# Moving a modulation product beside the first two down projections, and placing TensorE's operands at multiples of 2,048 bytes

## What is computed

```
h  = x + short_conv_mixer(rms_norm(x))          # in: 1024 -> 3*1024, width-3 convolution, out: 1024 -> 1024
h  = h + conv_ffn(rms_norm(h))                  # up 1024 -> 2*2816, convolution, silu(g)*u, down 2816 -> 1024
h  = h + mla_attention(rms_norm(h), shared_latent_kv(...), cos, sin)   # 8 heads
h  = h + conv_ffn(rms_norm(h));  x = rms_norm(h) * final_norm

mod = silu(c) @ w_ada + b_ada                   # 1 x 6144: shift, scale, gate, twice
h  = _rmsnorm(x, g_mix) * (1 + scale1) + shift1
x  = x + (1 + gate1) * (gating | stick-breaking | dilated window, of h @ w_in) @ w_out
h  = _rmsnorm(x, g_ffn) * (1 + scale2) + shift2
x  = x + (1 + gate2) * (silu(gate) * val) @ w_down
return _rmsnorm(x, g_final)
```

## The kernel before

| operands of TensorE's split matmuls | before | in the change |
|---|---|---|
| XH, XL, WH, WL | 128 | 0 |
| MH, ML (A_OUT), HH, HL (down), QXH, QXL (DQ) | 1,792 | 0 |
| CLH, CLL (UKV), OH, OL (WO) | 256 | 0 |

## Time and profile before

### The profile page before, as it was taken

One profiled execution on the slowest core, in us unless ns is written; L12 is line 12 of the kernel. 1 busy time (PEld: TensorE's weight loads), 2 busy tenths in 40 slices (PEclk: granted clock), 3 DMA queues, 4 the chain that ended last, 5 costly groups with the idle time before them and its releaser, 6 DMA issues.

```text
span 1875.5 us, 22480 instructions
## 1 busy us (share of the span) xinstructions
PE 1795.5 (96%) x7820; PEld 1422.5 (76%) x7820; DVE 1142.2 (61%) x1509; ACT 700.9 (37%) x975; POOL 405.1 (22%) x172
## 2 busy tenths in 40 slices
PE   7978999999999899999999999899999899999997
PEld 6756788888887676778888888688657688888885
DVE  6998877777224765567777522473855667777212
ACT  4112444444223335444444322332463444434221
POOL 3434300000444340120000144344201300000342
PEclk9999999999999999999999999899998899999998
DMA  7565433223333220022232233222100222232231
GB/s 266 212 212 186 172 101 100 97 93 101 101 101 98 67 93 1 32 90 94 99 100 90 97 105 101 94 89 90 56 1 13 78 90 92 98 101 89 102 101 67
DMA packets 52043, 186.32 MB, mean 99 GB/s; under 512 B 5776, under 2 KB 6032, under 8 KB 51856
## 3 DMA queue, kind: packets, MB, share of 16 engines
q1 hardware_dynamic: 50256, 180.90, 28.4%
q10 hardware_dynamic: 1728, 4.63, 0.7%
HBM read 183.41 MB, written 2.10 MB: 99 GB/s over the span
## 4 chain that ended last, share of the span: by engine, by line
PE 81%; DVE 13%; issue 2%; ACT 2%; DVEq 0%; DMA 0%; POOL 0%; ACTq 0%; SPq 0%
PE ps L1429 24%; PE ps L1431 24%; PE ps L1430 24%; DVE ada L966 4%; PE ps L1595 1%; PE ps L1592 1%; DVE TG L978 1%; PE ps L1613 1%; DVE RB L1055 1%; DVE rb L852 1%; PE ps L1649 1%; PE ps L1682 1%; PE ps L1603 1%; DVE acc L848 1%; DVE CU L990 1%
## 5 line engine op out<-in xcount | busy, mean ns | idle before, releaser
L462 POOL TENSOR_TENSOR WL<-raw,WH 128x1024 fp32r<-128x1024 f32 x159 | 394.1, 2479 | 1422.2 <-ACT WH L514 1422.2
L1429 PE MATMUL ps<-XH,WH 128*128 128x512 f32 x1560 | 616.6, 395 | 37.3 <-DVE XL L859 10.5
L1430 PE MATMUL ps<-XL,WH 128*128 128x512 f32 x1560 | 610.4, 391 | 0.0
L1431 PE MATMUL ps<-XH,WL 128*128 128x512 f32 x1560 | 610.3, 391 | 0.0
L514 ACT ACTIVATE WH<-raw 128x1024 fp32r<-128x1024 f32 x291 | 308.2, 1059 | 579.1 <-PE ps L1431 577.2
L1429 PEld LDWEIGHTS ps<-XH,WH 128*128 128x128 f32 x1560 | 294.8, 189 | 110.6 <-issue 19.5
L1431 PEld LDWEIGHTS ps<-XH,WL 128*128 128x128 f32 x1560 | 294.7, 189 | 62.2
L1430 PEld LDWEIGHTS ps<-XL,WH 128*128 128x128 f32 x1560 | 294.9, 189 | 60.9 <-issue 1.0
L1431 PE MATMUL ps<-HH,WL 128*128 128x512 f32 x528 | 208.6, 395 | 0.0
L1429 PE MATMUL ps<-HH,WH 128*128 128x512 f32 x528 | 208.6, 395 | 0.0
L1430 PE MATMUL ps<-HL,WH 128*128 128x512 f32 x528 | 208.5, 395 | 0.0
(11 more groups left out here) (257 smaller groups left out, 1877.5 us busy)
## 6 DMA issues: line engine op xcount, KB each, us to landing
raw<-w_tiles SPq DMA_DIRECT2D x291, 512.0 KB, 3.2
ada<-ada_tiles SPq DMA_DIRECT2D x48, 512.0 KB, 4.5
out_x<-X SPq DMA_DIRECT2D x8, 256.0 KB, 2.2
X<-x_in ACTq DMA_DIRECT2D x2, 512.0 KB, 8.4
X<-x_in SPq DMA_DIRECT2D x2, 512.0 KB, 8.8
MK<-mask_in ACTq DMA_DIRECT2D x1, 1024.0 KB, 4.8
crow<-c_in ACTq DMA_DIRECT2D x1, 512.0 KB, 11.5
cst<-const_in ACTq DMA_DIRECT2D x1, 384.0 KB, 13.2
```

The source lines that it names most:

```text
L462: nc.gpsimd.tensor_tensor(WL[k % SPL][:, :], raw[:, k, :], f32(WH[k % SPL][:, :]), ALU.subtract).then_inc(s_lo, 1)
L1429: mm(bank, h, xh, start=first, stop=False)
L1430: mm(bank, h, xl, start=False, stop=False)
L1431: return mm(bank, lo, xh, start=False, stop=last)
```

## The change

It has two parts. `adaln` leaves A_CH, A_B and A_OUT and stands ahead of `product(m)` in the residual loops of DN0 and DN1: three instructions for each of the 16 results m. Its tiles use three buffers: two in `ada01`, which lies over TG, TU, CG and CU (free in a down projection), and the third over cos and sin, which are now one tile `trig`, loaded behind DN0. `crow` lies over RA and RB (`RAB`), is loaded twice, and its silu moves into the first round of UP0 and of UP1. Lines 1004 to 1011 move behind DN1. `load_ada` issues three DMAs behind every third weight tile of a down projection, and waits for the product of m-1 first (for the first, for the last HL). Second, `align=LINE` (2,048) is given to X and all split operands, and the small tiles are declared first.

```
-ADA = 6
+ADA = 3
+LINE = 4 * S
...
+        XH = sb("XH", [P, KD, S], F32R, align=LINE)
+        WH = [sb(f"WH{i}", [P, TILE], F32R, align=LINE) for i in range(SPL)]
...
+        ada01 = sb("ada01", [P, 2, D], F32, st)
+        ADA_SLOT = (ada01[:, 0, :], ada01[:, 1, :], trig[:, :, :].rearrange("p a b -> p (a b)"))
+        crow = RAB[:, :, :].rearrange("p a b -> p (a b)")
...
+            def load_ada(n, m):
+                if m == 0:
+                    sp.wait_ge(s_hl, FF * (n + 1))
+                else:
+                    sp.wait_ge(s_ada, ADA * (KD * n + m))
+                for q in range(ADA):
+                    sp.dma_start(ADA_SLOT[q], ada_tiles[ADA * (KD * n + m) + q]).then_inc(s_ada_in[q], 16)
...
+                if t == T0["A_OUT"]:
+                    load_crow()
+                if t == T0["UP1"] + RAW:
+                    sp.wait_ge(s_ol, HEADS)
+                    load_crow()
+                for n in range(2):
+                    down = t - T0[f"DN{n}"]
+                    if down == 5:
+                        load_ada(n, 0)
+                    elif down >= 6 and down % 3 == 0 and down <= 3 * KD:
+                        load_ada(n, down // 3 - 1)
+                if t == T0["DN0"] + 3 * KD + 2:
+                    sp.wait_ge(s_ada, ADA * KD)
+                    for half in range(2):
+                        sp.dma_start(trig[:, half, :], rope_in[half]).then_inc(s_in["rope"], 16)
...
+            def adaln(n, i, k):
+                for q in range(ADA):
+                    a = i * (4 * ADA) + (ADA * (KD * n + k) + q)
+                    dve.wait_ge(s_ada_in[q], i * 64 + 16 * (KD * n + k + 1))
+                    w = ADA_SLOT[q]
+                    v.scalar_tensor_tensor(w, w, 1.0, crow, ALU.mult, ALU.mult, accum_out=dst).then_inc(s_ada, 1)
...
+                        if modulation is not None:
+                            adaln(modulation, i, k)
                         product(M, i, per)
...
-                    for q in range(3 * k, 3 * k + 3):
-                        adaln(i, q)
...
-            residual("A_OUT", 1, E_F0, "ffn_norm0", N_F0, beside=ada_beside)
-            dve.wait_ge(s_ada, 6 * KD)
+            residual("A_OUT", 1, E_F0, "ffn_norm0", N_F0)
...
+            residual("DN0", 3, E_KV, "kv_in", N_KV, modulation=0)
...
+            residual("DN1", 3, None, None, N_FIN, modulation=1, second=True)
+            dve.wait_ge(s_ada, 6 * KD)
```

More of the change, by code:

```diff
@@ L120, in build, with sb @@
     with ctx:
-        def sb(name, shape, dt=F32, stack=ctx):
-            return stack.enter_context(nc.sbuf_tensor(name, shape, dt))
+        def sb(name, shape, dt=F32, stack=ctx, align=32):
+            return stack.enter_context(nc.sbuf_tensor(name, shape, dt, align_bytes=align))
         def sem(name):
             return ctx.enter_context(nc.semaphore(name))
[L128 to L133, removed]
         vec = sb("vec", [P, -(-V["width"] // 16) * 16])
         cst = sb("cst", [P, C["width"]])
[L136 to L144, removed]
         mask16 = sb("mask16", [P, 3, P], BF16)
@@ L150, in build @@
         nt = sb("nt", [P, 8, 4])
+        X = sb("X", [P, KD, S], align=LINE)
+        XH = sb("XH", [P, KD, S], F32R, align=LINE)
+        XL = sb("XL", [P, KD, S], F32R, align=LINE)
+        raw = sb("raw", [P, RAW, TILE])
+        WH = [sb(f"WH{i}", [P, TILE], F32R, align=LINE) for i in range(SPL)]
+        WL = [sb(f"WL{i}", [P, TILE], F32R, align=LINE) for i in range(SPL)]
+        trig = sb("trig", [P, 2, S])
+        cos_t, sin_t = trig[:, 0, :], trig[:, 1, :]
+        rb = sb("rb", [P, S])
+        rbl = sb("rbl", [P, S])
+        acc = sb("acc", [P, S])
+        SQ = sb("SQ", [P, 2, S])
+        AT = sb("AT", [P, 2, S])
+        RAB = sb("RAB", [P, 2, S])
+        RA, RB = RAB[:, 0, :], RAB[:, 1, :]
         st = ExitStack()
         CV = sb("CV", [P, KD, S], F32, st)
[L155 to L158, removed]
+        MH = sb("MH", [P, KD, S], F32R, st, align=LINE)
+        ML = sb("ML", [P, KD, S], F32R, st, align=LINE)
         st.close()
         st = ExitStack()
[L161 to L166, removed]
+        HH = sb("HH", [P, FF, S], F32R, st, align=LINE)
+        HL = sb("HL", [P, FF, S], F32R, st, align=LINE)
+        st2 = ExitStack()
+        TG = sb("TG", [P, S + 16], F32, st2)
+        TU = sb("TU", [P, S + 16], F32, st2)
+        CG = sb("CG", [P, S], F32, st2)
+        CU = sb("CU", [P, S], F32, st2)
+        st2.close()
+        ada01 = sb("ada01", [P, 2, D], F32, st)
         st.close()
+        ADA_SLOT = (ada01[:, 0, :], ada01[:, 1, :], trig[:, :, :].rearrange("p a b -> p (a b)"))
+        crow = RAB[:, :, :].rearrange("p a b -> p (a b)")
         st = ExitStack()
-        QXH = sb("QXH", [P, KD, S], F32R, st)
-        QXL = sb("QXL", [P, KD, S], F32R, st)
+        QXH = sb("QXH", [P, KD, S], F32R, st, align=LINE)
+        QXL = sb("QXL", [P, KD, S], F32R, st, align=LINE)
         st.close()
@@ L599, in body @@
                         newest_tap(M + 1, i, CU, TU, jj + FF)
+                    if isinstance(i, int) and f < 2:
+                        act.wait_ge(s_in["c"], 16 * (f + 1))
+                        nc.scalar.activation(crow, crow, ACT.Silu).then_inc(s_cact, 1)
                 nc.scalar.preload_act_table(ACT.Silu)
@@ L1152, in _ @@
                 v.memset(rbl[:, half * (S // 2):(half + 1) * (S // 2)], 0.0).then_inc(s_acc2, 1)
-            residual("DN1", 3, None, None, N_FIN, second=True)
+            dve.wait_ge(s_cact, 2)
+            residual("DN1", 3, None, None, N_FIN, modulation=1, second=True)
+            dve.wait_ge(s_ada, 6 * KD)
+            b0 = V["b_ada"][0]
+            ch.link(v.tensor_tensor(mod[:, :], mod[:, :], vec[:, b0:b0 + 6 * KD], ALU.add))
+            for row, (part, g) in enumerate(((1, "g_mix"), (4, "g_ffn"))):
+                ch.step(v.scalar_tensor_tensor(gm[:, row, :], mod[:, part * KD:(part + 1) * KD], 1.0,
+                                               vec[:, V[g][0]:V[g][0] + KD], ALU.add, ALU.mult))
+            for row, part in ((2, 2), (3, 5)):
+                ch.link(v.tensor_scalar(gm[:, row, :], mod[:, part * KD:(part + 1) * KD], 1.0, None, ALU.add))
+            ch.link(v.tensor_tensor(gm[:, 0, :], gm[:, 0, :], vec[:, V["final"][0]:V["final"][0] + KD], ALU.mult))
             dve.wait_ge(s_ssum, N_FIN + 2)
```

54 lines of the change are left out of this document (10 added, 44 removed).

## The result

The changed kernel takes **1827.9 us** (median of 4 runs, 1825.5 to 1833.9), the kernel before 1873.8 us in the runs beside it (4 runs, 1869.7 to 1875.9): a ratio of 0.976, 95% interval 0.973 to 0.979, 45.9 us less between the medians. The profiled execution took 1833.86 us with a span of 1832.0, where that of before took 1877.21: 43.4 us less. It is the slowest of the changed kernel's four: its mean granted clock is 0.983, that of the others 0.985 to 0.988.

The account below looks back on a forecast made before the run. TensorE's matmul count and the distance between starts bound the kernel, except early, where VectorE's modulation products make it wait. First layer -32.3, new place 0, starts -10.5 and -2.0 give -44.8 us: 1872.6 to 1828 us, range 1745 to 1848.

Parts of the forecast that it names:

- A_CH to A_OUT: First layer, freed of the modulation's products: 210.3 us to become 178.0, 32.3 us less, at least 28.
- Rival 4: First layer: the weight's line, not the products, bounds it; only 10 of 32 us go, 1850 us; chance 0.03.
- Part 2: Products' new place beside DN0 and DN1: VectorE's idle time covers them, cost 0, bounds 0 to 4 us.
- rival 2: Operand starts do nothing and each phase keeps its pace: 1841 us; chance 0.08.
- SyncE's queue: DN0 and DN1: transfers waiting for products are issued some 9 us ahead of use; nothing is late.
- The start: Kernel's beginning: 1 MB less is transferred, worth 0 to 1 us, taken as 0.
- Part 3: Operand starts: all split matmuls run at 226.7 ns; 10.5 us less in down projections, 2.0 in DQ, UKV and WO.
- Reading (a): Split matmuls: stream and next weights' load collide in memory by relative position modulo 512; all run at 226.7 ns after the change.
- (b): Split matmuls: a row running across a multiple of 2,048 bytes costs extra, more if further off.
- Rival 1: All split matmuls reach 216 or even 213.3 ns: 1737 to 1758 us; chance 0.25 with 216 ns or less.
- Rival 3: Stream and weights fall on the same part of memory at each step, 240 ns for all: 1918 us; chance 0.06.
- that of DQ and UKV: DQ, UKV and WO: 384 matmuls each 5.1 ns shorter, 2.0 us in all, with WO's distance taken for all.

Follow-up runs that it names:

- experiment 8: Changed kernel plus one VectorE instruction of a product's size ahead of each result's first product in DN0 and DN1, 16 in all: 1830.4 us, ratio 0.977.
- experiment 3: Changed kernel with all split operands, weights included, starting 256 bytes past a multiple of 2,048: 1831.5 us, ratio 0.978.
- experiment 1: Changed kernel with the operand starts put back as before, so only the modulation is moved: 1841.7 us, ratio 0.983.
- experiment 5: Changed kernel with weights at 0, XH at 32, HH at 96, MH and QXH at 192, OH and CLH at 320 bytes: 1868.3 us.
- experiment 6: Changed kernel with weights at 0, XH at 256, HH at 448, MH and QXH at 160, OH and CLH at 224 bytes: 1840.4 us.
- experiment 9: Kernel of experiment 4, with only 64 of 128 weight columns loaded and used in blocks other than a tile's first and last: 1848.9 us.
- experiment 10: Changed kernel, all starts at 0, with only 64 of 128 weight columns loaded and used in blocks other than a tile's first and last: 1845.7 us.
- experiment 2: Kernel before with only the operand starts moved to multiples of 2,048, modulation left in the first layer: 1858.0 us, ratio 0.992.
- experiment 4: Changed kernel with weights at 0, XH at 128, HH at 256, MH and QXH at 384, OH and CLH at 64 bytes: 1866.8 us.
- experiment 11: Changed kernel with one half of a moving operand off: XL at 128 with XH at 0, HH at 128 with HL at 256: 1860.7 us.

## Why the prediction was right

**What bounded the kernel** was read rightly: with the products gone from the first layer nothing came in their place. A_CH to A_OUT took 178.5 us where 178.0 was forecast, and UP0 begins at 188.2 where 188 stood. Rival 4 (the weight's line bounds it) falls by that number.

**Part 2 at 0** is right: the modulation alone gives 1841.7 us, and rival 2's 1841 was the same sum. VectorE's wait shrank from 10.8 to 4.7 us, a little under the 5 to 6 forecast. One working was off without harm: I let a low half beside a product take 3.19 us. In DN0 GpSimd, which begins first, pays 0.2 us, and VectorE nearly all of it, the third product of most results 3.40 us:

```profile
526.75 2.57 POOL L489 TENSOR_TENSOR WL<-raw,WH 128x1024 fp32r<-128x1024 f32 x1 [3.12 <-ACT WH L538]
```

The low half had begun at 526.75, 0.25 us ahead of the product of 527.00, and ended at 529.32; the product ended at 530.40, 1.1 us behind that, as if it had run only then. The Trainium skill, "SBUF — State Buffer", section "Who interferes with whom", has it that the port pair of the two is an exclusive lock and that the order of issue decides who waits. These rows agree to 0.2 us, and so does the low half of experiment 8 that began second and took 3.30 us. So VectorE's idle time, not the 1.1 us to spare on GpSimd's side, is the limit of this place. SyncE's queue did what was worked out: the transfers for the next result are issued at 530.4 and 531.3 us and the first of them is used at 539.67, 9 us later. Those into `ada01` took 5.5 us at the median and 7.4 at most; of all 48 the longest took 8.2. The row is that of `ada01`:

```profile
DMA to landing us min/median/max: 3.2/5.5/7.4
```

The finalization behind DN1 went into the idle time as planned: VectorE now waits 2.17 us there instead of 3.07, and the next step comes no later.

```profile
1152.45 0.16 DVE L1176 TENSOR_SCALAR nt<-ps 128x4 f32<-128x4 f32 x1 [2.17 <-PE ps L1476]
```

The start gave 0.8 us where I took 0 of 0 to 1.

**Part 3.** Distances came out at 226.7 to 226.9 in DN0, DN1, DN2 and WO: -3.45 and -3.4 us in the first two, -4.1 from DN2 on (of which the distances are 3.5), and -1.1 in WO against 192 x 5.1 ns = 1.0. Reading (a) was right against (b) in that the start relative to the weights decides (experiment 3). Its picture of a collision in the memory isn't shown: 32 bytes apart cost as much as 128, and half a load made matmuls slower at 0 apart, which it doesn't explain. The Trainium skill, "SBUF — State Buffer", section "Who interferes with whom", gives the stream and the load independent read ports. Taken to mean that neither slows the other, that does not hold here: moving only the stream's start changes the pace, and halving only the load does so too. Rival 1 (216 ns) doesn't appear in any phase of float32r here; 226.7 was the lowest of all starts tried. The 215.7 ns of the Trainium skill, "TensorE: Matmul & The Clock Gate", section "Wait — 56ns, not 53.3ns?", is not reached either. Rival 3 (a collision at equal places) is the opposite of what the map shows. The modulus, 512 in the prediction, is 256; this changes none of its numbers, as 1,792 and 256 less 128 are 128 apart by both.

**The term that was mis-sized** is that of DQ and UKV: 1.0 us of the 2.0 was to come from them, and the two together became 1.1 us longer. Distances in DQ fell as forecast, from 232.9 to 227.1, but its granted clock stood at 0.90, where it had been 0.95; the first row is of the kernel before, the second of the changed one:

```profile
601.00:634.00 33.00, 27.89 (x110) 21.18 (x109) 28.91 (x30) 10.61 (x14) 10.90 (x6) 0.95 0.20 64
```

```profile
565.00:599.00 34.00, 28.49 (x109) 21.68 (x108) 29.91 (x30) 10.47 (x14) 10.66 (x6) 0.90 0.19 62
```

In the records the half clock lasts 6.8 us there, from 575.5 us, and 3.4 in the kernel before, both about the same wait of 3.0 us of TensorE for VectorE's sum of squares (`acc`). 3.4 us more at half the clock cost 1.7 us. The change isn't what lengthened it: at that wait, 2.97 to 3.01 us long in twelve of the traces, the half clock lasts 6.8 us in the changed kernel and in experiment 1, 3.4 in the kernel before and in experiments 3, 5, 6, 8, 9 and 10, and doesn't come in experiments 2, 4 and 11. Experiment 8 has the operands, the starts and the modulation of the changed kernel there, and its DQ took 30.5 us instead of 31.7. So 1.2 us of this miss is chance of one execution.

What is left is that DQ became 0.1 us shorter and not 0.5 (30.57 us before, 30.49 in experiment 8): TensorE waits 2.1 us behind it for a low half, where it waited 1.8. UKV hardly moved: its mean distance went from 232.3 to 230.6 ns only, though it is 0 apart too. Its matmuls stand in groups of at most 18 behind small matmuls of another kind, and the records show what that does: a group begins with distances mostly of 229 to 236 ns, and only behind five to nine of them does it come to 226 and 227 (from 613.94 us on, behind the first: 230, 236, 229, 232, 231, 227, 226, 227, 227, 226). The prediction took the pace of an unbroken phase for a broken one.

The two misses, +0.8 at the start and -2.1 here, nearly cancel. That the median fell on the forecast to 0.1 us is luck beyond that: the changed kernel's own four runs lie 8 us apart.

## What to carry to other kernels

Where matmuls with their own weight load run back to back, compare the distance between starts from phase to phase; if the same instruction has two paces, look at where its operands start relative to each other, and try stream and weights a multiple of 256 bytes apart (here 233.3 ns became 226.7, for a pad). Expect less where the matmuls stand in short groups. Work with no hurry belongs beside a long stretch whose engine has idle time in every period: subtract from that idle time what the work takes beside its neighbours there, not alone, and expect next to nothing to be lost below that and all that goes beyond it; look at the first period by itself, where idle time may not be there yet. Whether the halves of a change add is shown by a run of each alone.

## What was unexpected of the hardware

- Start of the stream against start of the weights counts modulo 256 bytes, with 226.7 ns at 0, 228.9 at 64, and 232.4 to 234.3 at 32, 96, 128, 160, 192 and 224.
- Loading 64 columns of weights instead of 128 made matmuls slower, 229.2 to 229.7 ns against 226.7 at the best start, and 230.0 among half loads alone.
- Behind the small matmuls between UKV's groups five to nine distances, mostly of 229 to 236 ns, come before 226.7 is reached, also at the best start.
- A misplaced operand has no one price: with XL alone at 128 the three up projections, with the same code of TensorE and the same addresses, ran at 231.1, 233.3 and 228.9 ns.
- An operation of VectorE of 128x1024 that began 0.25 us behind GpSimd's subtraction of the same size took 3.40 us instead of 1.21, the subtraction 2.57 instead of 2.40. Where the subtraction began 0.16 us behind such an operation, it took 3.30. The later one bears nearly all of the delay, so that the same instruction costs a result 1.2 or 3.4 us by a quarter of a microsecond.
